# Weight parts laid out in rows 32 bytes longer, so that the parts of the value projections begin 32 bytes off a multiple of 64, and one matrix of constants fewer

## The reference, cut to what matters

```
for l in range(2):
    xn = rmsnorm(x, norm_mix[l])
    (qa, ka, va, qb, kb, vb, qc, kc, vc, qi, ki, wi, gates) = split(xn @ w_in[l])
    o_a = chunk_band_attention(qa, ka, va)
    o_b = diff_attention(qb, kb, vb)        # ends in a root-mean-square norm over 128 channels
    o_c = dsa_attention(qc, kc, vc, qi, ki, wi)
    y = g0 * (o_a @ w_up_a[l]) + g1 * (o_b @ w_up_b[l]) + g2 * (o_c @ w_up_c[l])
    x = x + y @ w_out[l]
    x = x + memory_cross_attention(...)
    x = x + swiglu(rmsnorm(x, norm_ffn[l]), w_gu[l], w_down[l])
```

## Time and profile before

| | |
|---|---|
| median of three runs | 1608.95 us (1607.92 to 1609.51) |
| the profiled execution: its own time | 1607.3 us |
| its span, first to last instruction | 1605.2 us |
| granted TensorE clock, mean | 0.991 of full speed |
| TensorE busy | 1563.0 us, 97% of the span |
| VectorE busy | 880.4 us, 55% |
| ScalarE busy | 647.6 us, 40% |
| GpSimd busy | 58.0 us, 4% |
| DMA | 245 GB/s over the span |

### The profile page before, as it was taken

One profiled execution on the slowest core, in us unless ns is written; L12 is line 12 of the kernel. 1 busy time (PEld: TensorE's weight loads), 2 busy tenths in 40 slices (PEclk: granted clock), 3 DMA queues, 4 the chain that ended last, 5 costly groups with the idle time before them and its releaser, 6 DMA issues.

```text
span 1605.2 us, 25930 instructions
## 1 busy us (share of the span) xinstructions
PE 1563.0 (97%) x11055; PEld 1261.9 (79%) x11055; DVE 880.4 (55%) x1302; ACT 647.6 (40%) x1024; POOL 58.0 (4%) x28
## 2 busy tenths in 40 slices
PE   9999999899889999999999999999999999999998
PEld 8886434334444359989899899999989999899998
DVE  6943212112121148677877676647576878576653
ACT  2034212202202135464654554435464674554443
POOL 0000000000000000033000000000006000000000
PEclk9999999999999999999999999999999999999999
DMA  9177999999999995646244456474653543465550
GB/s 351 52 314 302 383 420 427 429 428 427 430 427 428 427 403 206 197 143 200 106 158 158 151 169 206 158 266 158 197 187 121 175 158 132 127 211 180 166 210 27
DMA packets 130086, 393.86 MB, mean 245 GB/s; under 512 B 4672, under 2 KB 60352, under 8 KB 117952
## 3 DMA queue, kind: packets, MB, share of 16 engines
q1 hardware_dynamic: 129984, 392.39, 64.9%
HBM read 386.34 MB, written 1.05 MB: 241 GB/s over the span
## 4 chain that ended last, share of the span: by engine, by line
PE 82%; DVE 9%; DMA 7%; issue 1%; ACT 1%; SPq 0%; DVEq 0%; ACTq 0%
PE psum L1343 12%; PE psum L1063 11%; PE psum L1064 11%; PE psum L1071 11%; DMA ring<-w 6%; PE psum L1425 5%; DVE outs L2119 3%; PE psum L1728 2%; PE psum L1726 2%; PE psum L1729 2%; PE psum L1305 2%; PE psum L1579 2%; PE psum L1524 1%; PE psum L1525 1%; PE psum L1523 1%; PE psum L1023 1%
## 5 line engine op out<-in xcount | busy, mean ns | idle before, releaser
L1063 PE MATMUL psum<-h_parts,w_hi 128*128 128x256 f32 x1472 | 364.7, 286 | 1.2 <-DVE w_lo L662 1.2
L1064 PE MATMUL psum<-h_parts,w_lo 128*128 128x256 f32 x1472 | 355.1, 279 | 0.0
L662 DVE TENSOR_TENSOR w_lo<-raw_a,w_hi 128x1024 fp32r<-128x1024 f32 x186 | 225.1, 1222 | 113.1 <-ACT w_hi L1748 112.1
L1063 PEld LDWEIGHTS psum<-h_parts,w_hi 128*128 128x128 f32 x1472 | 276.1, 188 | 13.7 <-issue 10.6
L1064 PEld LDWEIGHTS psum<-h_parts,w_lo 128*128 128x128 f32 x1472 | 277.5, 189 | 0.2
L1748 ACT ACTIVATE w_hi<-raw_a 128x1024 fp32r<-128x1024 f32 x202 | 210.7, 1055 | 159.8 <-PE psum L1071 64.9
L1071 PE MATMUL psum<-h_parts,w_hi 128*128 128x256 f32 x1472 | 201.9, 279 | 0.0
L1343 PE MATMUL psum<-ring,outs 128*64 128x512 f32 x704 | 168.4, 626 | 20.5 <-DMA ring<-w 20.5
L1071 PEld LDWEIGHTS psum<-h_parts,w_hi 128*128 128x128 f32 x1472 | 184.6, 188 | 0.0
L1343 PEld LDWEIGHTS psum<-ring,outs 128*64 128x64 f32 x704 | 57.2, 144 | 124.4 <-issue 124.4
L662 DVE TENSOR_TENSOR w_lo<-raw_b,w_hi 128x1024 fp32r<-128x1024 f32 x92 | 111.4, 1221 | 53.0 <-ACT w_hi L1748 52.7
(11 more groups left out here) (318 smaller groups left out, 2535.0 us busy)
## 6 DMA issues: line engine op xcount, KB each, us to landing
ring<-w SPq DMA_DIRECT2D x70, 2048.0 KB, 15.9
raw_a<-w_in SPq DMA_DIRECT2D x20, 2048.0 KB, 8.3
raw_a<-w_gu SPq DMA_DIRECT2D x32, 1024.0 KB, 7.7
raw_b<-w_in SPq DMA_DIRECT2D x10, 2048.0 KB, 8.9
wp<-w SPq DMA_DIRECT2D x8, 2048.0 KB, 17.9
hs<-w SPq DMA_DIRECT2D x8, 2048.0 KB, 22.2
raw_b<-w_gu SPq DMA_DIRECT2D x12, 1024.0 KB, 7.1
raw_a<-w_down SPq DMA_DIRECT2D x8, 1536.0 KB, 6.4
```

The source lines that it names most:

```text
L662: return eng.tensor_tensor(chunk_part(w_lo, n), chunk_raw(n), chunk_part(w_hi, n).bitcast(F32), ALU.subtract)
L1063: mm(to, hi[:, k, :], h_hi[:, k, :], start=(k == 0), stop=False)
L1064: mm(to, lo[:, k, :], h_hi[:, k, :], start=False, stop=False)
```

## The change

The rows of the four buffers grow by 8 numbers (32 bytes), and `chunk_part` picks the start within a row: chunks of the values begin 32 bytes off a multiple of 64 in both parts, in whichever of the four buffers they fall, and all other chunks begin on a multiple of 64. `mean_sub` is left out of the constants; its sums are made with `mean_model`, and ScalarE multiplies them by D / (2 * CH) = 8 as it takes the root.

```diff
-for _name, _width in (("ident", P), ("mean_model", P), ("mean_mixb", P), ("mean_head", P), ("mean_sub", P),
+for _name, _width in (("ident", P), ("mean_model", P), ("mean_mixb", P), ("mean_head", P),
                       ("rotate", P), ("before", P), ("ones", P), ("cos", SEQ), ("sin", SEQ), ("mask", SEQ),
                       ("iota", SLOTS), ("first", PER_GROUP)):
...
-        w_lo = sb("w_lo", [P, PARTS, KD * P], F32R)
-        w_hi = sb("w_hi", [P, PARTS, KD * P], F32R)
+        w_lo = sb("w_lo", [P, PARTS, KD * P + H_SHIFT], F32R)
+        w_hi = sb("w_hi", [P, PARTS, KD * P + H_SHIFT], F32R)
...
         def chunk_part(parts, n):
             i, _ = chunk_source(n)
             dims = (2, HALF) if is_values(i) else (4, 2 * P) if LAYER_PIECES[i][0] == "up" else (KD, P)
-            return view(parts[:, BUFFER[n], :], 0, *dims)
+            return view(parts[:, BUFFER[n], :], H_SHIFT if is_values(i) == (BUFFER[n] % 2 == 0) else 0, *dims)
...
-                                last = mm(duo("subln")[:, at:at + 2], sq[:, k, t * P:(t + 1) * P], c("mean_sub")[:, 0:2],
+                                last = mm(duo("subln")[:, at:at + 2], sq[:, k, t * P:(t + 1) * P], c("mean_model")[:, 0:2],
...
-                        f(sub_roots, duo("subln")[:, 0:16], ACT.Sqrt, bias=eps[:]).then_inc(std_ready, 1)
+                        f(sub_roots, duo("subln")[:, 0:16], ACT.Sqrt, bias=eps[:], scale=D / (2 * CH)).then_inc(std_ready, 1)
```

## The result

The changed kernel takes **1618.3 us** (median of four runs, 1617.99 to 1620.88) against 1608.43 us for the kernel before (four runs, 1607.4 to 1609.51). The ratio is 1.0059, with a 95% interval of 1.0046 to 1.0071: slower by some 9.9 us. The prediction was 1610.4 us with a range up to 1613.0, so it is wrong: it forecast +1.4 us, and the loss is seven times that. The profiled execution of the changed kernel took 1618.25 us.

What follows compares the result with a forecast made beforehand. TensorE was taken to bound the kernel. The values' +1.4 us, with all other terms 0, added to the median of 1608.95 us gave 1610.4 us, range 1605.8 to 1613.0.

Steps and rivals of the forecast that it cites:

- What bounds the kernel: Whole kernel: TensorE, busy 97% of the span; in the second network other engines' work counts only through TensorE's waits.
- Part 1: Values projections: 288 matmuls get operands with equal starts and slow down by 5 ns each, +1.4 us.
- L1305's loss at equal starts: Experts, 256 columns: both operands 32 bytes off take 120.0 ns a matmul, 3.3 ns slower than with different starts.
- The row that I leaned on: Experts' matmuls at L1305, 256 columns, equal starts: 32 take 3.84 us, 120.0 ns each.
- Part 2: All chunks but the values, 6672 matmuls: starts within 64 bytes stay, so cost 0; bounds +11.0 and -33 us.
- the far bits count: slower: Rival, chance 0.08: buffers 1 and 2, 64 bytes off a multiple of 128, cost 3336 matmuls 3.3 ns each, +11.0 us.
- Parts 3, 4 and 5: Writing values' parts 32 bytes off, the scaled root with mean_model, one matrix less to load: 0 each; bounds +0.5, -0.8 us for the last two.
- The rule of the Trainium skill: TensorE's SBUF reads: independent ports for moving and stationary operands, so the values' cost would be 0, 1608.95 us.
- the untested bits: Starts of buffers 1 and 2 beyond 64 bytes: chance 0.10 of mattering, 0.08 slower and 0.02 faster.
- one coincidence: Values at a start difference of -32 and other chunks at +32 have one pace, taken as grounds for cost 0.

Runs made afterwards that it cites:

- e7: Kernel before with H_SHIFT 0 and without mean_sub: activations in h_parts start like the weights modulo 256 bytes (distance 0); 1622.3 us, ratio 1.0082.
- e6: Kernel before without mean_sub, both weight parts 64 bytes later, activations moved by 512 (all distances, activations' start minus weights' modulo 256, are 224); 1616.63 us, ratio 1.0054.

## Why the prediction was wrong, point by point

- *What bounds the kernel*: right. TensorE's pace alone moved the end, and the waits stayed.
- *Part 1, the values slow down by 5 ns*: wrong in sign. They gained 2.7 ns on average against before, 0.8 us in all. The step that failed was to carry L1305's loss at equal starts from 256 to 512 moving columns; at 512 an equal start is a good one (227.3 ns in e7). Besides, the starts were made equal modulo 64, and in most of the chunks not modulo 256. The row that I leaned on was true for its own shape only: at 256 columns e7 shows 120.3 ns at a distance of 0, as L1305 had.
- *Part 2, all other chunks at 0*: this is the step that cost the prediction. "I take 0, because the values today have the difference of starts negative (-32) and the others positive (+32) and both have one pace, which a longer period would leave to chance": it was chance. At 256 columns a distance of 224, which is -32, costs 118.2 ns (e6), so -32 is not the equal of +32; the values' 233.1 at -32, with 512 columns, only looked like twice 116.7. In its place: 6672 matmuls slower. The time lost in the second network, 9.3 us, and the values' 0.8 us the other way make 10.1 us, 1.5 ns a matmul: 1.9 in gate and up, 2.8 in down and less in the shorter stretches.
- *The rival "the far bits count: slower"* (0.08, 1620 us) is what happened, with 1618.3 us. Its mechanism was right and its parts were off, so that its number came this near partly by luck: it had buffers 1 and 2 pay 3.3 ns and the others nothing. Buffers 1 and 2 pay 2.3 in the runs of L1071, buffer 3 pays 1.8 and buffer 0 0.3, and in L1063 and L1064 all four pay 1.0 to 1.4. I had left out that `w_lo` grows by 128 bytes and so moves all of `w_hi`.
- *Parts 3, 4 and 5* held. GpSimd's parts take 2403 ns off a multiple of 64 as on it, ScalarE's and VectorE's busy times are those of before, and e1, with the constants' part alone, has a ratio of 0.9997.
- *The rule of the Trainium skill* ("TensorE: Matmul & The Clock Gate", section "Step-by-step: what each phase is for"), two independent read ports for the moving and the stationary operand: by itself it would have the starts of the two not matter to each other. The runs say that they do: the matmuls of the down projection take 113.2 to 120.1 ns as their activations are moved against the weights. The measurement decides here; whether the two operands meet at the ports or elsewhere, no run shows.
- The range was too narrow at the top because I gave the untested bits 0.10 in all, while the argument for leaving them at 0 was one coincidence.

## What to carry to other kernels

Where TensorE is the bound and streams float32r, the distance of the two operands modulo 256 bytes is a parameter of the kernel like a tile size: it is worth up to 7 ns of 117 for each matmul, its good values depend on the number of moving columns and on what the stream before did, and any tensor that grows ahead of either operand changes it for all that lies behind. Pad such a tensor by multiples of 256 bytes, or measure again. A loss of this kind appears in no wait and no count, only in the time from one matmul's start to the next.

## What the hardware did that I had not expected

A float32r matmul of 256 columns took 113.2 ns to 120.3 ns at one granted clock (1.00) as the distance of its operands changed, with a period of 256 bytes as far as nine distances show. At one distance there can be several steady paces for the same instructions (113 and 118 ns at 64; 113, 117 and 119 ns at 16), and which one a stream runs at depends on what ran before it: a stream keeps its pace until a pause or other matmuls break it.
